# A streaming encoder layer on one core: the first expert's rows built by a one-hot product instead of a DRAM gather

## What is computed

```
logits = h @ w_router + b_router;  top 4 of 32 experts per token;  gates = softmax(top values)
for each expert e, over the rows of h routed to it:
    gu = rows @ w_gu[e] + b_gu[e];  gate, up = halves of gu
    gate = min(gate, 7);  up = clip(up, -7, 7)
    out = (gate * sigmoid(1.702 * gate) * (up + 1)) @ w_down[e] + b_down[e]
y = LN2(alpha * h + sum over the 4 experts of gate * out)
```

## Time and profile before

| | us |
|---|---|
| median of 3 runs (1258.63 to 1259.38) | 1259.34 |
| the profiled execution, whole | 1259.37 |
| its span, first to last instruction | 1257.0 |
| TensorE busy in it | 1192.7 (95%) |
| VectorE busy in it | 1049.4 (83%) |
| ScalarE busy in it | 944.6 (75%) |

### The profile page before, as it was taken

How to read it: one execution, slowest core, us unless ns; L and a number is a source line. 1 busy time by engine, 2 the same in 40 slices (tenths; PEclk the granted TensorE clock), 3 DMA queues, 4 the chain that set the end, 5 groups by cost and what they waited for, 6 DMA issues and landing times.

```text
span 1257.0 us, 35029 instructions
## 1 busy us (share of the span) xinstructions
PE 1192.7 (95%) x15369; PEld 867.1 (69%) x15369; DVE 1049.4 (83%) x1209; ACT 944.6 (75%) x1260; POOL 172.2 (14%) x145
## 2 busy tenths in 40 slices
PE   7999998899999999999999999999999999999995
PEld 3555455777777777777777777777777777677752
DVE  6564577998899889898898898888888888888888
ACT  6532313688889888888888898888888888788841
POOL 1273111111000100000000011111111111111002
PEclk9999997899999999999999999999999999999998
DMA  9752491899999999999999999999999999999994
GB/s 367 291 197 86 144 406 36 355 406 421 426 425 424 424 427 424 424 425 426 425 425 425 424 426 424 424 425 426 424 426 424 425 424 425 422 422 426 409 395 139
DMA packets 47670, 475.17 MB, mean 378 GB/s; under 512 B 8781, under 2 KB 9812, under 8 KB 21660
## 3 DMA queue, kind: packets, MB, share of 16 engines
q1 hardware_dynamic: 35432, 438.69, 83.1%
q0 software_dynamic: 11392, 31.77, 6.7%
q10 hardware_dynamic: 692, 2.43, 0.5%
HBM read 453.17 MB, written 29.95 MB: 384 GB/s over the span
## 4 chain that ended last, share of the span: by engine, by line
PE 49%; DMA 28%; DVE 12%; issue 5%; ACT 5%; POOL 0%; DVEq 0%; SPq 0%; POOLq 0%; ACTq 0%
PE wide L1017 34%; DMA ring<-in_w_gu 16%; PE pair L1017 14%; DMA ring<-in_w_down 11%; DVE work L1892 6%; ACT work L875 3%; PE pair L1347 1%; ACT work L905 1%; DVE ring L1994 1%; DVE ring L2019 1%; DVE ring L2017 1%; DVE work L1877 0%; DMA ring<-in_x_t 0%; DVE ring L2006 0%; DMA work<-h_rows,work 0%
## 5 line engine op out<-in xcount | busy, mean ns | idle before, releaser
L1892 DVE SCALAR_TENSOR_TENSOR work<-ring,work 128x2048 f16<-128x2048 f32 x320 | 721.4, 2287 | 109.4 <-ACT work L875 94.5
L875 ACT ACTIVATE work<-ring 128x2048 f16<-128x2048 f32 x320 | 599.6, 1902 | 90.5 <-DMA ring<-in_w_gu 55.6
L1017 PE MATMUL wide<-work 128*128 128x96 f16 (+2 forms) x6970 | 465.2, 227 | 28.5 <-issue 12.6
L1017 PEld LDWEIGHTS wide<-work 128*128 128x128 f16 (+2 forms) x6970 | 364.7, 101 | 112.6 <-issue 42.2
L1017 PE MATMUL wide<-ring,work 128*96 128x512 f32 (+4 forms) x1024 | 335.1, 492 | 1.4 <-DMA ring<-part_rows 1.4
L1017 PEld LDWEIGHTS pair<-work 128*128 128x128 f16 (+2 forms) x6483 | 297.0, 100 | 34.6 <-issue 23.7
L1017 PE MATMUL pair<-work 128*128 128x96 f16 (+3 forms) x6483 | 303.5, 208 | 8.2 <-DVEq L1727 1.9
L1017 PEld LDWEIGHTS wide<-ring,work 128*96 128x96 f32 (+4 forms) x1024 | 132.0, 135 | 178.3 <-issue 125.6
L678 POOL DMA_INDIRECT work<-h_rows,work x32 | 58.4, 1826 | 477.7 <-PE pair L1347 450.4
L691 POOL DMA_INDIRECT part_rows<-work x30 | 43.1, 1438 | 373.2 <-ACT work L935 373.2
L905 ACT ACTIVATE work<-pair,work 128x96 f32<-128x96 f32 x256 | 64.8, 333 | 0.0
(11 more groups left out here) (211 smaller groups left out, 599.1 us busy)
## 6 DMA issues: line engine op xcount, KB each, us to landing
ring<-in_w_gu SPq DMA_DIRECT2D x128, 2048.0 KB, 29.9
ring<-in_w_down SPq DMA_DIRECT2D x64, 2048.0 KB, 30.7
part_rows<-work POOLq DMA_DIRECT2D x1, 10240.0 KB, 37.2
ring<-part_rows SPq DMA_DIRECT2D x5, 2048.0 KB, 31.4
ring<-in_w_in SPq DMA_DIRECT2D x3, 2048.0 KB
ring<-in_w_out SPq DMA_DIRECT2D x2, 2048.0 KB, 10.8
h_rows<-work POOLq DMA_DIRECT2D x1, 2560.0 KB, 9.9
ring<-h_rows SPq DMA_DIRECT2D x5, 512.0 KB, 20.0
```

Source lines behind the costliest of these rows:

```text
L875: act.activation(whi[buf(n, p)], packed(s, p), ACT.Copy, scale=W_UP).then_inc(hi_done, 1)
L1017: return pe.matmul(out, w, x, start=start, stop=stop, skip_group_check=True)
L1892: dve.scalar_tensor_tensor(wlo[buf(n, p)], packed(s, p), W_UP, whi[buf(n, p)], ALU.mult, ALU.subtract).then_inc(split_done, 1)
```

## The change

TensorE multiplies each tile of h, still in SBUF, with a one-hot matrix of expert 0's places (`hot0`, float32, 96 columns) and sums over the tiles in PSUM: 8 float32 products of 128 x 128 x 96 a tile (`first_rows_of`). VectorE makes each tile's `hot0` after its rank (`first_pick`). The gather of expert 0, `first_ids` and the product before it go. The products of tiles 0 to 3 stand between `h_columns(4)`, `positions`, `logits(4)`, in place of two groups of idle products. On VectorE the one-hot of tile 4, the last gates, the two tables' copies and `onehot(1)` move behind the first splits; the tables of experts 0 and 1 move in between TensorE's units. SyncE issues (0, 4) and (0, 5) when the last tile is mixed and b_gu after the rows are in PSUM.

```diff
 SyncE, after the first six pieces
-            sp.wait_ge(hT_ready, 2 * TILES)
-            sp.wait_ge(h_stored, 16 * TILES)
-            sp.dma_start(bguT[:, 0:E, :], b_gu).then_inc(late_in, 16)
             sp.wait_ge(mix_ready, TILES)
-            sp.wait_ge(gathered[0], 16)
             for i in (4, 5):
                 load(0, i, piece_slot(0, i))
+            sp.wait_ge(h_stored, 16 * TILES)
+            sp.wait_ge(gT_ready, 2)
+            sp.dma_start(bguT[:, 0:E, :], b_gu).then_inc(late_in, 16)
 GpSimd
-                pool.wait_ge(rows_known, m + 1)
+                pool.wait_ge(rows_known, m)
...
-            gather(0, 0, 0)
 ScalarE
             act.activation(small[:, 91:92], small[:, 64:65], ACT.Sigmoid)
+            rows_hi(0, 0)
             act.wait_ge(h_stored, 16 * TILES)
             for p in range(2, BUFS):
                 next_hi(0, p)
-            rows_hi(0, 0)
 TensorE
+            def first_rows_of(t):
+                n = ROWS[t]
+                pe.wait_ge(pick_made, t + 1)
+                pe.wait_ge(h_done, t + 1 if t + 1 < TILES else t + 2)
+                for b in range(2):
+                    for k in range(4):
+                        last = mm(rows_bank(0, b)[:, k * BLK:(k + 1) * BLK],
+                                  xn[t][0:n, (4 * b + k) * P:(4 * b + k + 1) * P], hot0[0:n, t, :],
+                                  t == 0 and k == 0, t == TILES - 1)
+                    if t + 1 == TILES:
+                        last.then_inc(gT_ready, 1)
             pe.wait_ge(mix_used, TILES - 1)
-            idle(6)
+            first_rows_of(0)
+            first_rows_of(1)
             h_columns(TILES - 1)
             positions(TILES - 2)
+            first_rows_of(2)
             logits(TILES - 1)
-            idle(4)
+            first_rows_of(3)
             positions(TILES - 1)
+            pe.wait_ge(mix_used, TILES)
             idle(3)
-            pe.wait_ge(hot_ready, 1)
-            for t in range(TILES):
-                n = ROWS[t]
-                last = mm(bank[0][:, 488:489], hot[0:n, t, :], info[0:n, t, 0, 3:4], t == 0, t == TILES - 1)
-            last.then_inc(ids_ready, 1)
-            idle(4)
+            first_rows_of(TILES - 1)
...
-            table(0, 0)
-            table(1, 1)
-            idle(3)
-            rows(0, 0, 16, 2)
             for n in range(E):
                 for u in range(8):
                     unit(n, u, n % 2)
                     if n == 0 and u == 3:
-                        pe.wait_ge(bias_ready, 1)
+                        table(0, 0)
+                    if n == 0 and u == 5:
+                        table(1, 1)
+                    if n == 0 and u == 7:
+                        pe.wait_ge(table_copied, 2)
                         select(0)
 VectorE
+            def first_pick(t):
+                n = ROWS[t]
+                in_place = iota16[0:n, :].rearrange("p (g d) -> p g d", d=4)[:, :, 0:3]
+                dve.tensor_scalar(hot0[0:n, t, :].rearrange("p (g d) -> p g d", d=3), in_place, rank[0:n, t, 0:1],
+                                  None, ALU.is_equal).then_inc(pick_made, 1)
...
-            first_hot([TILES - 1]).then_inc(hot_ready, 1)
-            gate_info(TILES - 1)
-            dve.nop().then_inc(hot_ready, 1)
...
+            next_lo(0, 0)
+            rows_lo(0, 0)
+            dve.wait_ge(h_stored, 16 * TILES)
+            next_lo(0, 1)
+            first_hot([TILES - 1])
+            gate_info(TILES - 1)
+            dve.nop().then_inc(hot_ready, 2)
+            step(dve.memset(sig_bias, SWISH * LIMIT))
+            step(dve.memset(up_bias, 2 * LIMIT * S_UP))
+            next_lo(0, 2)
+            dve.wait_ge(late_in, 16)
+            dve.tensor_scalar(bguT[:, 0:E, :], bguT[:, 0:E, :], -S_UP, LIMIT * S_UP, ALU.mult, ALU.add)\
+               .then_inc(bias_ready, 1)
+            next_lo(0, 3)
+            step(dve.tensor_copy(used16, used[:, 0:BLK]))
             rows_of(0, 0, None)
             onehot(1, 1)
             rows_of(1, 1, None)
-            step(dve.memset(sig_bias, SWISH * LIMIT))
-            step(dve.memset(up_bias, 2 * LIMIT * S_UP))
-            next_lo(0, 0)
-            rows_lo(0, 0)
-            next_lo(0, 1)
-            dve.wait_ge(late_in, 16)
-            step(dve.tensor_copy(used16, used[:, 0:BLK]))
-            dve.tensor_scalar(bguT[:, 0:E, :], bguT[:, 0:E, :], -S_UP, LIMIT * S_UP, ALU.mult, ALU.add)\
-               .then_inc(bias_ready, 1)
-            next_lo(0, 2)
-            next_lo(0, 3)
             places_of(0, 0)
```

More of the change, by code:

```diff
@@ L190, in build @@
         bguT = take((E + 1) * 16, A + PLACES).rearrange("p (e f) -> p e f", f=16)
-        pick, pick_g = [take(TOPK * E, dec_at + 3456 + i * TOPK * E).rearrange("p (k e) -> p k e", k=TOPK)
+        pick, pick_g = [take(TOPK * E, dec_at + 6400 + i * TOPK * E).rearrange("p (k e) -> p k e", k=TOPK)
                         for i in range(2)]
@@ L204, in build @@
         cursor[0] = A + 2304
+        hot0 = take(TILES * BLK, dec_at + 6688).rearrange("p (t s) -> p t s", t=TILES)
         g1 = take(4 * BLK).rearrange("p (c s) -> p c s", c=4)
@@ L338, in build @@
         ov_place = sem("ov_place")
-        ids_ready, ln2_in = sem("ids_ready"), sem("ln2_in")
+        pick_made, ln2_in = sem("pick_made"), sem("ln2_in")
         y_done, y_stored = sem("y_done"), sem("y_stored")
@@ L402, in z_bank, with rows_bank @@
             return banks[2 + i % 2]
+        def rows_bank(m, b):
+            return wide[1][:, 512 * b:512 * b + 512] if isinstance(m, int) and m == 0 else bank[b]
         def total_bank(t):
@@ L898, in rows_hi @@
                     act.wait_ge(gT_ready, m * 2 + (b + 1))
-                    act.activation(xhi[q][:, 4 * b:4 * b + 4, :], bank[b][:, 0:4 * BLK]
+                    act.activation(xhi[q][:, 4 * b:4 * b + 4, :], rows_bank(m, b)[:, 0:4 * BLK]
                                    .rearrange("p (k s) -> p k s", k=4), ACT.Copy, scale=X_UP).then_inc(gT_hi, 1)
@@ L1239, in idle @@
                 for _ in range(count):
-                    mm(wide[1][:, 512:1024], oh[:, 1, 0:P], oh[:, 0, 0:512], True, True)
+                    mm(wide[0][:, 512:1024], oh[:, 1, 0:P], oh[:, 0, 0:512], True, True)
             def h_columns(t):
@@ L1265, in positions @@
                 n = ROWS[t]
-                o = (banks[3] if t + 1 < TILES else wide[1])[0:n, 0:E]
+                o = banks[3][0:n, 0:E]
                 if t:
                     pe.wait_ge(routed, t)
[L1269 to L1272, removed]
+                    pe.wait_ge(ranked, t)
                 for s in range(t):
@@ L1339, in rows @@
                 pe.wait_ge(table_copied, tables)
-                if not isinstance(m, int) or m > 0:
-                    pe.wait_ge(dst_known, m)
-                    select(m)
+                pe.wait_ge(dst_known, m)
+                select(m)
                 pe.wait_ge(gathered[q], got)
@@ L1422, in _ @@
                 if n + 1 < E:
-                    rows(n + 1, (n + 1) % 2, 16 * ((n + 1) // 2 + 1), min(n + 3, E))
+                    rows(n + 1, (n + 1) % 2, 16 * ((n + 2) // 2), min(n + 3, E))
                 down(n, [piece_slot(n, 4), piece_slot(n, 5)], [landed(n, 4), landed(n, 5)])
@@ L1432, in _ @@
                     table(b + E, e)
-                    rows(b + E, 0, b * 16 + 16 * (E // 2 + 1), b + (E + 1))
+                    rows(b + E, 0, b * 16 + 16 * (E // 2), b + (E + 1))
                     for u in range(16):
@@ L1697, in first_hot @@
                 return last
-            def first_ids():
-                dve.wait_ge(ids_ready, 1)
-                dve.tensor_scalar(tok_i[0], bank[0][:, 488:489], float(PLACES), None, ALU.add).then_inc(rows_known, 1)
+            def first_pick(t):
[3 more added lines that the diff above has]
+                                  None, ALU.is_equal).then_inc(pick_made, 1)
             def gate_info(t):
@@ L1712, in gate_info @@
                 step(dve.tensor_tensor(each_g, each, g4.unsqueeze(2).to_broadcast([n, TOPK, E]), ALU.mult))
-                if t + 1 == TILES:
-                    first_ids()
                 step(dve.tensor_reduce(gate, each_g.rearrange("p k e -> p e k"), AX.X, ALU.add))
@@ L1724, in rank_tile @@
                 dve.wait_ge(pos_ready, t + 1)
-                o = (banks[3] if t + 1 < TILES else wide[1])[0:n, 0:E]
+                o = banks[3][0:n, 0:E]
                 step(dve.scalar_tensor_tensor(rank[0:n, t, 0:E], o, 1.0, member[0:n, t, :], ALU.add, ALU.mult))
                 dve.nop().then_inc(ranked, 1)
+                first_pick(t)
             step(dve.memset(iota16, -1.0))
@@ L1882, in rows_lo @@
                     dve.wait_ge(gT_hi, m * 2 + (b + 1))
-                    dve.scalar_tensor_tensor(xlo[q][:, 4 * b:4 * b + 4, :], bank[b][:, 0:4 * BLK]
+                    dve.scalar_tensor_tensor(xlo[q][:, 4 * b:4 * b + 4, :], rows_bank(m, b)[:, 0:4 * BLK]
                                              .rearrange("p (k s) -> p k s", k=4), X_UP,
```

## The result

| | before | after |
|---|---|---|
| median of 6 runs each (lowest to highest) | 1258.81 (1256.65 to 1259.38) | 1267.22 (1265.88 to 1269.17) |
| profiled execution, whole | 1259.37 | 1265.88 |
| its span | 1257.0 | 1264.1 |

The change makes the kernel slower: ratio 1.0071, 95% interval 1.0058 to 1.0083. The forecast of 1262.1 had the sign, but the time lies outside its range of 1256.2 to 1264.5.

A forecast was written before the change was run, and what follows sets the result against it. The prediction took the weight stream to bound the kernel, restarting at the issue of piece (2, 1). That slips 3.85 us, less 1.15 gives 2.7; 1259.37 + 2.7 = 1262.1 us, range 1256.2 to 1264.5.

The forecast's parts named there:

- the stream's shift: Weight stream: restarts at the issue of piece (2, 1), so it ends later by that issue's slip less 1.15: 2.7 us.
- The slip of (2, 1): SyncE's issue of weight piece (2, 1), after expert 0's compute: later by 2.7 + 1.15 = 3.85 us.
- The last rank: TensorE's path before expert 0: products ahead delay it 3.6 us at half clock, 1.4 at full; 2.7 taken.
- From there to pair 4: VectorE's list from the last rank: 20.2 us at half clock, 1.15 more than before; 19.05 at full.
- its sign of being wrong: SyncE: the forecast is wrong if weight piece (2, 1) is issued before 262 us.
- The credit of 1.15: Weight stream at piece (2, 1): 2.1 us of queued transfers gone, less 0.95 us to restart an idle stream.
- just covered: TensorE, tiles 0 and 1: products take 4.4 us, hidden because `positions(3)` waited until 209.98 anyway; cost 0.
- The wait for `select`: VectorE before pair 4: a new wait of some 1.7 us, as `table(1)` and `select` depend on TensorE's units 6 and 7.
- Part of 210 to 217 at full: TensorE's clock before the last rank: partly full between 210 and 217 us, so the rank slips 2.7 us.
- The first rival: TensorE holds the full clock from 207 us: stream shift 0.25, 1259.6 us, no change; chance 0.32.
- The second: Expert 0 not held by VectorE: units and `down` move with the first unit, 1256.2 or 1252.8 us; chance 0.18.
- The third: Half clock throughout: stream 3.6 us later, 1263.0, up to 1264.5; chance 0.50 for slower together with the forecast.

The follow-up runs named there:

- e2: The kernel before with 104 empty TensorE instructions in the never-entered branch, putting the code boundary where the changed kernel has it: 1265.18 us, ratio 1.0049.
- s2: The changed kernel with pieces (0, 4) and (0, 5) issued only after the rows are in PSUM: 1266.34 us, ratio 1.0053 to the kernel before.
- e1: The changed kernel with 152 empty TensorE instructions in the never-entered branch, putting the code boundary back to 119: 1259.77 us, ratio 1.0007 to the kernel before.
- e4: The kernel before with 120 empty TensorE instructions in the never-entered branch, so the whole tail lies in one code block: 1259.45 us, ratio 1.0000.
- m1: The changed kernel with 226 empty instructions in the never-entered branch, boundary some 45 instructions into the tail: 1260.77 us, ratio 1.0007 to the kernel before.
- s5: The changed kernel, 151 idle instructions in the branch, tile 0's product moved ahead of `h_columns(3)`: 1266.19 us, ratio 1.0049 to the kernel before.
- s1: The kernel before with only the change's SyncE order, pieces (0, 4) and (0, 5) issued early: 1258.77 us, ratio 1.0000.
- s4: e1 with the wait for the table's copy and `select(0)` moved ahead of units 6 and 7: 1257.57 us, ratio 0.9987 to the kernel before.

## Why the prediction was wrong, point by point

**The step that failed is the sum.** It set 1259.37 + 2.7, the stream's shift, and so took everything behind the experts as merely moved. It had no term for where code lies. The stall and the half clock after it are about 6 us (e2: +6.2; s2 less e1: 6.6; after less e1: 7.5, from different groups). With that term, 1262.1 would have been 1268; the measured median is 1267.22. What the profile before could have shown: its chain has 1.43 us of "issue" at 1217.12, right behind a branch, so something that is not work already had a price there, and about 104 instructions were to be put ahead of it. By e4 this is another stall than the one that followed, so it was a hint and not a source for the 6 us. The Trainium skill ("Runtime: NRT & Kernel Launch", "Instruction fetch mechanics") says that a taken branch to a target outside the fetched window stalls until its block is there, and that crossing a block's end otherwise is "mostly hidden". The first could account for the stall at the tail's first product, but that one is 1.43 us in one profile and absent in others, so it is not shown. The second does not hold just behind the branch here, with 4.64 us in after and 4.15 in e2; 45 and 119 instructions on it does, with 0.36 us and nothing.

**The stream's shift, 2.7, was right in sign, and its size is not borne out.** It is 2.35 in the first pair of profiles, but e1 and m1, whose tails lose little or nothing, are only 0.9 us over the kernel before (-0.3 to 2.0 each). If the 0.2 to 1.6 us that the latter loses at its tail's first product are added, the shift is 1.1 to 2.5. In part the agreement with 2.35 is luck:
- The slip of (2, 1) was put at 3.85; it was 2.58. The last rank slipped by 2.4 (2.7 taken), 1.8 of it by the change. From there to pair 4 it took 18.3 us, not 20.2 as at the half clock or 19.05 as at the full. Then 0.9 us came that no term had, with the half clock at 238.6 to 245 inside expert 0, after TensorE had stood waiting for pairs. In e1 and s2 they are missing, and there (2, 1) goes out at 261.32 and 261.77, before the 262 that the prediction named as its sign of being wrong.
- The credit of 1.15 (2.1 us of backlog less 0.95 of restart) was put on (2, 1). The 0.95 is the time to the first packets and not to full engines, and so was the row it was read from: behind the issue at 224.20 they move 82 GB/s from 225.4 to 226. Within 10 us of its issue of (2, 1) after moves 3.5 MB (242 GB/s for 4 us, then 421), before 4.0 (401); at 424 GB/s this is 1.2 us where 0.95 was taken. Of the credit, the table leaves 0.1 to 0.4 against the profile before. Against the other two with the old order of pieces, e2 (944.1) and e4 (945.6), it would be more, so single profiles don't settle it. At 290 to 305 us after moves 395 GB/s and before 419 (0.36 MB, 0.85 us), but e2 has 409 and e4 395 there, so this dip is not the change's. What makes it stays open.

**Sizes of single terms.** 16 records of 96 columns took 2.00 us at the full clock and 3.71 at half (s5), 0.125 and 0.23 each; 0.11 and 0.165 were taken. At half the bound from 128 columns (0.22) was the right one, not three quarters of it. Tiles 0 and 1 were held "just covered" at 4.4 us; they took 6.6 (5.5 in e1) and were not. The wait for `select`, about 1.7, measured 1.83.

**The clock.** "Part of 210 to 217 at full" was too careful for that stretch (0.97 from 210.4 to 220.2), and the clock was overlooked at 207 to 210, which was at full before and is at half now. The first rival's full clock from 207 did not come.

**The early pieces.** That their late start costs little is borne out by s1 and s2; the 2.1 us, or 1.15 net, are not seen. (0, 4) went out at 198.3 (201 forecast), (1, 2) at 225.0 (226).

**The rivals.** The first, no change at 1259.6, is where e1 lands (1259.77) once the stall is out. But it is so by another way: the clock was at half from 207 to 210, and (2, 1) slipped by 1.1 us and more. The second said that the first unit would carry everything; it came 4.5 us earlier and carried nothing, because TensorE then waited 2.33 and 1.50 us for VectorE. Its point of decision, VectorE's wait behind units 6 and 7, was well chosen: s4 takes that wait away and is faster than the kernel before. The third, a stream shift of 3.6 or more, was not reached in after; s5 shows how it would look. Landing times at 500 us fell from 24.0 to 20.4. The engines slipped by more (4.4 us, the down pieces at 518.79 for 514.42) than the stream (2.35), which explains 2.0 of the 3.6:

```profile
ring<-in_w_gu SPq DMA_DIRECT2D x4, 2048.0 KB, 20.4
```

**What remains of the change.** With the code in a good place e1 is 0.9 us over the kernel before (-0.3 to 2.0), which is not told from no change: the stream's cost, less whatever the kernel before loses at its tail's first product (0.2 to 1.6 us in the profiles). With `select` earlier it wins 1.4. The change as made is slow for the most part because of where code lies, which its logic did not cause.

## What to carry to other kernels

When an edit adds or removes instructions ahead of a jump, look at what stands right behind it: "issue" idle in the middle of a group whose operands are there may be code arriving, and idle instructions in the branch not taken tell in one run whether it is. In a kernel bound by a stream, find the one issue after which the stream never stands still again, and price every edit by what it does to that issue. Before a shift of 2 us is read off a pair of profiles, look at how far two executions of the same code lie apart. A step moved earlier brings nothing while the next engine's list decides; here the gather's removal alone brought nothing that can be measured (e1), and moving one wait two units forward brought some 2 us (s4 against e1).

## What was not expected of the hardware

- A block boundary 15 instructions behind a jump's target costs 4.15 to 4.64 us and then some products at half clock, 6 us in all. The second block comes 5.5 to 6 us after the first (q8 from about 1216.5 and 1222.5 in after), while weights fill the DMA engines (436 GB/s from 1218 to 1222.5). That the load causes the 6 us is not shown.
- A second, smaller stall at the jump's target varies from one execution to the next, 0.24 and 1.43 us with the same TensorE code (s1, before).
- TensorE 94% busy over 27.5 us was granted half clock all the time (s5), its records filling 210.4 to 220.2 without a gap, and 97% busy at 238.6 to 245 in after it had half clock too. The Trainium skill ("TensorE: Matmul & The Clock Gate", "Why this matters for your kernels") has the full clock come with gapless work; s5's filled stretch and that of the kernel before speak against that for these mixes of short float32 and half-precision products.
